# Rebuilding the second attention stage of a hybrid encoder layer: no PE transposes of the values, normalisation and gating moved out of the loop, values one step later

## Time and profile before

| | |
|---|---|
| median of 3 runs | 2778.05 us |
| profiled execution | 2780.88 us, span 2779.1 us |
| PE busy | 2647.0 us (95% of the span) |
| DVE / ACT / POOL busy | 1269.1 / 1065.1 / 373.8 us |
| DMA queue of SP | 362.03 MB, 48.8% of 16 engines |
| mean granted TensorE clock | 0.964 |

### The profile page before, as it was taken

The page is one execution under the profiler, slowest core; times in us unless marked ns, Lnnn a source line. Parts: engine busy times, 40 slices in busy tenths (PEclk is TensorE's granted clock), DMA queues, the critical chain, the costliest instruction groups (busy, mean ns, idle before and its releaser), DMA issues.

```text
span 2779.1 us, 39778 instructions
## 1 busy us (share of the span) xinstructions
PE 2647.0 (95%) x14546; PEld 2320.9 (84%) x14546; DVE 1269.1 (46%) x2638; ACT 1065.1 (38%) x2225; POOL 373.8 (13%) x257
## 2 busy tenths in 40 slices
PE   7999999999999999989999998884999999999997
PEld 5888888998888889989999988884788888888886
DVE  5211146141111363278877876786333433343333
ACT  4111122131111221278888877775222222222222
POOL 2000000000000000000000002333233233323331
PEclk9999999999999999999999987786999999999998
DMA  6431246363222363698876668766433333343330
GB/s 201 147 122 64 79 107 145 131 227 129 108 85 73 90 127 131 167 213 198 194 183 160 161 162 187 184 171 157 137 95 92 101 107 93 88 106 105 95 87 38
DMA packets 331191, 364.49 MB, mean 131 GB/s; under 512 B 83496, under 2 KB 253752, under 8 KB 326840
## 3 DMA queue, kind: packets, MB, share of 16 engines
q1 hardware_dynamic: 330168, 362.03, 48.8%
q0 software_dynamic: 896, 0.80, 0.1%
HBM read 227.88 MB, written 135.93 MB: 131 GB/s over the span
## 4 chain that ended last, share of the span: by engine, by line
PE 72%; issue 9%; DVE 9%; DMA 5%; SPq 2%; ACT 2%; POOL 1%; DVEq 0%; POOLq 0%; ACTq 0%
PE psum L1333 71%; DVE pt_lo L1143 5%; DMA g_b<-g_d 2%; DMA av<-v_d 1%; PE psum L1550 1%; POOL y_b L693 1%; DMA yb_d<-y_b 1%; DVE prob L1127 1%; DVE small L1127 1%; SPq L310 1%; SPq L438 0%; ACT prob_b L874 0%; PE psum L1496 0%; SPq L603 0%; DVE y_b L1208 0%
## 5 line engine op out<-in xcount | busy, mean ns | idle before, releaser
L1333 PE MATMUL psum<-x_hi,w_hi 128*128 128x512 f32 x1408 | 549.5, 390 | 18.4 <-DVE x_lo L1029 17.8
L1333 PE MATMUL psum<-x_lo,w_hi 128*128 128x512 f32 x1408 | 549.1, 390 | 0.0
L1333 PE MATMUL psum<-x_hi,w_lo 128*128 128x512 f32 x1408 | 549.0, 390 | 0.0
L693 POOL TENSOR_TENSOR y_b<-y_b,g_b 64x512 f32<-64x512 f32 x64 | 89.6, 1401 | 1776.2 <-DVE y_b L1208 1637.5
L1333 PEld LDWEIGHTS psum<-x_hi,w_hi 128*128 128x128 f32 x1408 | 265.1, 188 | 73.7 <-issue 17.8
L1333 PEld LDWEIGHTS psum<-x_lo,w_hi 128*128 128x128 f32 x1408 | 265.1, 188 | 55.2
L1333 PEld LDWEIGHTS psum<-x_hi,w_lo 128*128 128x128 f32 x1408 | 265.0, 188 | 54.9
L1127 DVE CUSTOM_DVE_ANT_0 prob<-psum,bias 128x640 f32<-128x640 f32 (+4 forms) x256 | 199.1, 778 | 86.2 <-issue 85.9
L1333 PE MATMUL psum<-wo_hi,y_hi 128*128 128x512 f32 x512 | 204.1, 399 | 31.9 <-DVE y_lo L1238 27.0
L839 ACT ACTIVATE prob<-prob,small 128x640 f32<-128x640 f32 (+4 forms) x256 | 204.0, 797 | 66.0 <-DVE small L1127 66.0
L1143 DVE TENSOR_TENSOR pt_lo<-psum,pt_hi 128x640 fp32r<-128x640 f32 (+4 forms) x256 | 199.2, 778 | 8.6 <-ACT pt_hi L848 8.6
(11 more groups left out here) (163 smaller groups left out, 5140.8 us busy)
## 6 DMA issues: line engine op xcount, KB each, us to landing
qk_d<-stage_out SPq DMA_DIRECT2D x80, 512.0 KB, 2.8
w_raw<-in_w_in SPq DMA_DIRECT2D x24, 1024.0 KB, 5.7
x_raw<-in_xT SPq DMA_DIRECT2D x32, 512.0 KB, 4.7
g_d<-stage_out SPq DMA_DIRECT2D x64, 256.0 KB, 2.0
bq_d<-stage_out SPq DMA_DIRECT2D x64, 256.0 KB, 4.0
v_d<-stage_out SPq DMA_DIRECT2D x32, 512.0 KB, 3.1
ya_d<-y_a SPq DMA_DIRECT2D x128, 128.0 KB, 3.6
bq<-bq_d SPq DMA_DIRECT2D x64, 256.0 KB, 4.3
```

The lines of the kernel that those rows point to most:

```text
L693: pool.tensor_tensor(yb, yb, g_b[:, s, :, :].rearrange("p h t -> p (h t)"), ALU.mult).then_inc(by_gated, 1)
L1333: return pe.matmul(dst, lhs, rhs, start=start, stop=stop)
```

## The change

Stage B is rebuilt, and what it took over from or leaves to its neighbours changes with it:

- Projection: the 8 A value heads and 2 B value heads are one block of 640 columns, two panels of 320, all token by feature into `v_d`. The B value units (4 per half, 512 wide) go; each of the 32 token-major products per half is 320 wide instead of 256.
- B loads its values straight from `v_d`, tokens on partitions, into a resident `v_b` (one 2 MB DMA per group instead of two of 0.5 MB); `b_v` and L889 go.
- Probabilities are no longer normalised. Row sums and shifts are kept for all units (`b_sum`, `b_shift`); after steps 50 and 66 the sink's exponential, sum and reciprocal are made for half of the sequence at once, transposed by PE and stored to `r_d`. Transposes wait for the exponentials alone.
- Values are made for two units at once (`b_values(d, part)`): per chunk three matmuls with 64 stationary and 256 moving columns, two chunks per step, at lags 7 and 8 from the first unit's scores (6 before). DVE copies a pair's output every second step (64x1024), SP stores it; POOL has nothing to do in B.
- C: gate and reciprocal are applied to all 8 column blocks in `y_tile`: two of POOL's three operations go from 512 to 1024 columns, `g_c` and `r_c` are twice as large. `mix(1)` moves ahead of PE's wait for all weight strips.
- Hand-over: tile 0 is loaded at step 57, tile 1 at step 61, eight strips before step 55; ACT and DVE split tile 0 at step 64 and one strip in each of steps 64 to 71.

```diff
-COL_QK, COL_G, COL_BQ, COL_BK, COL_BV, COL_AV = 0, 1024, 2048, 2560, 2688, 2816
+COL_QK, COL_G, COL_BQ, COL_BK, COL_V = 0, 1024, 2048, 2560, 2688
+V_HEADS = A_HEADS + B_KV
+VP = V_HEADS // 2
+VW = VP * HEAD
...
@@ SP
             def load_bv(kv, s):
-                for c in range(2):
-                    cols, src = kv_rows(ROW_BV, kv, s, c)
-                    sp.dma_start(bvt[c * HEAD:c * HEAD + HEAD, s, cols], src).then_inc(bv_loaded[s], 16)
...
+                sp.dma_start(v_b[:, s, n0:B_HALF // CHUNK, :].bitcast(f32),
+                             bass.AP(tensor=v_d.tensor, offset=first,
+                                     ap=[[row, P], [CHUNK * row, B_HALF // CHUNK - n0], [1, P]])
+                             ).then_inc(bv_loaded[s], 16)
...
+            def store_yb(d):
+                pair, s, i = b_unit(2 * d)
+                t0 = s * B_HALF + 4 * i * CHUNK
+                sp.wait_ge(by_copied, d + 1)
+                sp.dma_start(yb_d[pair * P:pair * P + 4 * HEAD, t0:t0 + 4 * CHUNK].rearrange("(h d) t -> d h t", d=HEAD),
+                             y_b[:, d % 2, :, :]).then_inc(by_stored[d % 2], 16)
...
+                if step == 3 * GROUP + 9:
+                    for stored in by_stored:
+                        sp.wait_ge(stored, 16 * (3 * B_UNITS // 2 + 1))
+                    sp.wait_ge(brecip_stored, 16 * 4)
                     load_tile(0, 0)
+                    load_x(0, 0)
+                if step == 3 * GROUP + 13:
+                    load_tile(1, 1)
+                if B_ALL + 4 <= step < B_ALL + 7:
+                    n = step - B_ALL + 4
+                    sp.wait_ge(cw_split, n - 4)
+                    load_strip(n)
...
+                if step >= 10 and step % 2 == 0 and step // 2 - 5 < B_DOUBLES:
+                    store_yb(step // 2 - 5)
+
+            sp.wait_ge(bvalues_done, B_DOUBLES)
+            for n in range(KT + 3, KT + 7):
+                load_strip(n)
+            for stored in by_stored:
+                sp.wait_ge(stored, 16 * (B_DOUBLES // 2 + 1))
+            load_strip(KT + 7)
...
@@ POOL
-                pool.tensor_tensor(y_raw[:, s, 0:KT // 2, :], y_raw[:, s, 0:KT // 2, :], g_c[:, s, :, :], ALU.mult
+                pool.wait_ge(y_loaded[s], 8 * (t - s) + 16)
+                pool.tensor_tensor(y_raw[:, s, :, :], y_raw[:, s, :, :], g_c[:, s, :, :], ALU.mult
                                    ).then_inc(y_ready, 1)
@@ ACT
-                    act.activation(small[:, 48 + 4 * q:52 + 4 * q], small[:, 16 + 4 * q:20 + 4 * q], ACT.Exp,
-                                   bias=sink_sb[:, 0, pair:pair + 1], scale=1.0).then_inc(bexp_done, 1)
...
-                    act.activation(v_b[:, u // 2 % 4, :, :].rearrange("p c d -> p (c d)"), psum[:, 7, :],
-                                   ACT.Copy).then_inc(bv_ready, 1)
...
-                    act.activation(yb_low[:, u % 2, :], psum[HEAD:P, 4 + u % 3, :], ACT.Copy).then_inc(by_low_ready, 1)
...
             for step in range(B_ALL + B_DRAIN):
                 b_step(step)
-                if B_ALL <= step < B_ALL + DRAIN_STRIPS:
+                if step == B_ALL:
+                    y_tile_hi(0, 0, True)
+                if B_ALL <= step < B_ALL + KT:
                     strip_hi(step - B_ALL)
@@ DVE (in b_step; denominator, reciprocal and normalisation per unit are gone)
+                if step % 2 == 1 and 0 <= step - 9 and (step - 9) // 2 < B_DOUBLES:
+                    d = (step - 9) // 2
+                    dve.wait_ge(bvalues_done, d + 1)
+                    dve.wait_ge(by_stored[d % 2], 16 * (d // 2 + 1))
+                    dve.tensor_copy(y_b[:, d % 2, :, :].rearrange("p h (c q) -> p h c q", q=CHUNK),
+                                    psum[0:HEAD, 4 + 2 * (d % 2):6 + 2 * (d % 2), :]
+                                    .rearrange("p a (c h q) -> p h (a c) q", h=4, q=CHUNK)).then_inc(by_copied, 1)
@@ PE
             def b_transpose(u):
-                pe.wait_ge(bnormed, u + 1)
+                pe.wait_ge(bexp_done, u + 1)
...
+            def b_values(d, part):
+                pair, s, i = b_unit(2 * d)
+                if part == 0:
+                    pe.wait_ge(bprobsT_split, 2 * d + 2)
+                    if d >= 2:
+                        pe.wait_ge(by_copied, d - 1)
...
+                for c in range(2 * part, 2 * part + 2):
+                    dst = psum[0:HEAD, 4 + 2 * (d % 2) + part, c % 2 * 2 * P:(c % 2 + 1) * 2 * P]
+                    ph, pl = (t[:, d % 3, c, :, :].rearrange("p u q -> p (u q)") for t in (ptb_hi, ptb_lo))
+                    vh, vl = (v_b[:, s, 4 * i + c, x:x + HEAD] for x in (0, HEAD))
+                    mm(dst, vh, ph, True, False)
+                    mm(dst, vh, pl, False, False)
+                    last = mm(dst, vl, ph, False, True)
...
             for step in range(-1, B_ALL + B_DRAIN):
-                for fn, lag in ((b_values, 6), (b_transpose, 3), (b_v, 3), (b_scores, -1)):
-                    if 0 <= step - lag < B_ALL:
-                        fn(step - lag)
+                v = step - 7
+                if 0 <= v < B_ALL:
+                    b_values(v // 2, v % 2)
...
+                if 0 <= step - 3 < B_ALL:
...
+                    b_transpose(step - 3)
+                if step + 1 < B_ALL:
+                    b_scores(step + 1)
...
             mix(0, 0)
             transpose_h(0, 0)
+            mix(1)
             pe.wait_ge(cw_split, 2 * KT + 2)
```

More of the change, by code:

```diff
@@ L395, in _ @@
                     if j == 1:
[L396 to L400 removed]
+                        next_panel(12, COL_V + VW, VW)
                 for w in range(2):
[L402 to L405 removed]
@@ L581, in _ @@
                     load_bk(1, group - 1, (since - 1,))
-                if group in (1, 2) and since == 5:
-                    sp.wait_ge(bv_done, B_UNITS * group)
+                if group in (1, 2) and since == 8:
+                    sp.wait_ge(bvalues_done, B_UNITS * group)
                     load_bv(1, group - 1)
@@ L773, in panel @@
                                 split_w(pbase + w + 1, i, 1 - slot, next_width)
-                        if last and half == 0:
-                            for c in x_after(r):
+                        if last and half == 0 and r % 2 == 1:
+                            for c in x_after(r // 2):
                                 split_x(1, c)
@@ L861, in _, with y_tile_hi, b_sinks, b_recip_copy @@
                            ).then_inc(recipT_copied, 1)
+            def y_tile_hi(t, s, first=False):
+                act.wait_ge(y_ready, t + 1)
+                if not first:
+                    act.wait_ge(mix_done, t)
+                act.activation(y_hi[:, :, :], y_raw[:, s, :, :], ACT.Copy).then_inc(y_hi_done, 1)
+            def b_sinks(s):
+                act.wait_ge(bexp_done, (3 + s) * 2 * B_UNITS)
+                for pair in range(B_HEADS // 2):
+                    cols = slice(s * P + pair * 32, s * P + pair * 32 + 32)
+                    last = act.activation(b_shift[:, cols], b_shift[:, cols], ACT.Exp, bias=sink_sb[:, 0, pair:pair + 1],
+                                          scale=1.0)
+                last.then_inc(bsink_done, 1)
+            def b_recip_copy(s):
+                act.wait_ge(brecipT_done, s + 1)
+                act.activation(recipb_t[:, s, :], psum[:, 3, 0:P], ACT.Copy).then_inc(brecipT_copied, 1)
             def b_step(step):
+                if step in (B_RECIP0, B_RECIP1):
+                    b_recip_copy(step == B_RECIP1)
                 u = step - 1
@@ L1239, in y_tile_lo @@
                                   ).then_inc(y_split, 1)
+            for step in range(B_ALL + B_DRAIN):
+                b_step(step)
+                if step == B_ALL:
+                    y_tile_lo(0, 0)
+                if B_ALL <= step < B_ALL + KT:
+                    strip_lo(step - B_ALL)
+            LN0 = CHAINED + 6
+            LN_STEPS = 8
             def p_tile_lo(t, s):
```

457 lines of the change are left out of this document (198 added, 259 removed).

## The result

The changed kernel takes 2739.83 us (median of 4 runs, 2737.41 to 2742.88); the kernel before, on the same chip, 2779.91 (2776.28 to 2782.74). The ratio is 0.9857, 95% interval 0.984 to 0.9874: 1.4% faster. The forecast was 2700 us, 2.8% faster, with a range of 2655 to 2745. The sign and the range held; the gain came out at half its size. The profiled execution took 2737.41 us, its span 2735.6.

A forecast was written before the change was run, and what follows sets the result against it. The prediction saw a chain of stalls in stage B and its hand-over, not one bound. Terms -2.5 - 48 - 29 + 1 = -78.5 took 2780.9 to 2702.4, less 2.8 for the median: 2700 us, range 2655 to 2745.

The forecast's parts named there:

- B's units, -48: Stage B's 64 units: 193 us in place of 241, from 155 for the first 48 and 38 for the last 16.
- The bound from compute: Stage B's loop over engines: 2.33 us per unit at full clock, 116 us for the first 48 units.
- DMA bound of 143: Stage B's first 48 units: moving 33.7 MB, values at 266 GB/s and the rest at 231, takes 143 us.
- the last 16: Stage B's last units: no keys or queries to wait for, 38 us with reciprocal block and tile loads.
- The bursts still stall it: Rival, chance 0.20: in stage B bulk loads ahead of stores keep DMA at 188 GB/s, 180 us; total 2725.
- The lag: Stage B: the values' added step of lag is hidden by their own slack and costs one step of drain.
- Drain, -29: From B's last exponentials to the start of mix(0, 0): 15 us in place of 44.
- Start of C, +1: From mix(0, 0) to the residual the second transposes need: +1 us, between -6 and +8.
- Stage C, 0: Stage C's loop: POOL's wider operations add 2.2 us a tile, within 3.1 of cover; 0.9 remain, 0 us.
- Stage C slips: Rival, chance 0.05: POOL slower by a factor of 2.2, each tile 6.4 us late, 192 us; total 2892.
- Stage A, "otherwise untouched": Stage A: only moved by a half of the projection moved into it, otherwise untouched; 0 us.
- Projection, -2.5: Projection on PE: B value units removed, 768 matmuls widened from 256 to 320 columns; -2.5 us for both halves.

The follow-up runs named there:

- e5: Changed kernel with stage B's later key and value loads spread over more steps in smaller DMAs, same bytes; 2730.23 us, ratio 0.9822.
- e10: Changed kernel plus DVE's residual first, ACT's waits swapped, one lag step less, B's loads spread, tile 2's loads earlier, PE's stage A loop written out; 2690.44 us.
- e6: Changed kernel without stage B's query, key and value loads after the first group (only its time counts); 2712.45 us, ratio 0.9750.
- e12: e10 with the loads of tiles 0 and 1 split over nine steps, r_c first, a store between them; 2686.58 us, ratio 0.9660.
- e11: e6 with the added step of lag in stage B undone as in e4 (only its time counts); 2703.28 us, ratio 0.9698.
- e4: Changed kernel with only the added step of lag in stage B undone; 2728.08 us, ratio 0.9812.
- e9: Changed kernel with tile 2's loads right behind the last strips and POOL's wait for constants moved to its first scaling; 2731.53 us, ratio 0.9808.
- e1: Changed kernel with ACT's y_hi waiting first for the mix, then for POOL's y; 2731.05 us, ratio 0.9814.
- e3: Changed kernel with 64 semaphore increments at the start of PE's program, moving stage A's loop down the code; 2734.11 us, ratio 0.9826.
- e8: Changed kernel plus DVE's residual first, ACT's waits swapped, one lag step less, tile 2's loads before the last two strips, PE's A loop written out; 2701.78 us.

## Why the prediction was right in stage B and wrong outside it

**B's units, -48: measured -46.3, by two errors that cancel, which is luck.** The bound from compute was sound: 2.35 us per unit without the loads against 2.33, and 113.7 us for the 48 units against 116. For the first 48 units 155 us were taken between a DMA bound of 143 and a ceiling; they took 140.9. That this is near 143 is luck too. The bound was priced at 231 GB/s, and it is none: spread, the same bytes moved at 247 GB/s and the 48 units took 129.4 us (e5) and 127.3 (e10), so the changed kernel loses 12 us there to its bursts. For the last 16, which "have no keys or queries to wait for", 38 us were taken, and they took 51. The forecast had tile 0's loads there only as something that might be late, not as something that holds up the output stores queued behind them. e6 and e12 show that stall. The rival *The bursts still stall it* had the right mechanism, but at 180 us for the 48 units a price far too high.

**The lag.** "The added step of lag for the values is hidden by their own slack": true of the steady loop (e11), but it counted the step at one step of drain, and it cost 4 us there and another 3 to 5 in the last units (e4, e11).

**Drain, -29: measured -25.1.** PE waited 5.0 us for a low part that stood behind tile 0's split and one weight strip, and DVE's work was not all as counted. Four strips were priced at 1.2 us each; the one here took 3.37 and the next 1.65, beside two operations of POOL on tile 1 that took 3.40 and 3.17 us in place of 2.34 (POOL, DVE, DVE, PE):

```profile
1858.81 3.40 POOL L727 TENSOR_TENSOR g_c<-g_c,r_c 128x1024 f32<-128x1024 f32 x1 [7.33 <-DMA r_c<-r_d]
...
1859.92 3.37 DVE L1240 TENSOR_TENSOR wo_lo<-strip_a,wo_hi 128x1024 fp32r<-128x1024 f32 x1
1863.22 0.68 DVE L1199 TENSOR_TENSOR ptb_lo<-psum,ptb_hi 128x512 fp32r<-128x512 f32 x1
...
1864.04 1.09 PE L1491 MATMUL psum<-ident,prob_b 128*128 128x128 f32 x4 [5.01 <-DVE ptb_lo L1199]
```

The prediction looked for DVE and POOL in each other's way in stage C, where POOL's operations keep their 2.39 to 2.40 us, and not in the drain, where the long operations stand side by side. In e9, where that strip takes 1.22 us and a later one 2.78, PE's longest wait is 4.0 us and the drain 18.6 in place of 19.2, so this explains a part of the 4 us; no run was made to take the two apart.

**Start of C, +1: measured +8.1.** The strips were all split 24.5 us after the start of `mix(0, 0)`, as predicted. But the prediction sets these 24.5 against 20.9 before and says that the rest follows as now, which makes +3.6; no working stands behind its +1. What also failed is "tile 2 and its three POOL operations follow as now": from there to tile 1's residual it took 26.6 us, not 21.1. POOL's two wider operations are 2.1 of that and the table load 1.3; the rest is put down to the loads, with twice as much for `g_c` and `r_c`, which is argued and not shown. That the second mix ahead wins nothing was right: tile 2's y stands in front of tile 1's residual on DVE.

**Stage C, 0: measured +9.8. This is the step that failed outright.** The cover of 3.1 us, the 2.2 us that POOL takes of it and the 0.9 that remain were read from an even tile. In an odd one the removed wait for `y_loaded` on ACT had changed which wait the table load stands behind, and 1.28 is more than 0.9 (e1: with the load back under the wait, 710.7 us). The rival *Stage C slips* looked at the right loop, but for a slower POOL; POOL's wide operations are 2.39 to 2.40 us in the rows above, as priced.

**Stage A, "otherwise untouched": measured +7.7.** Untouched source isn't untouched code: with 388 fewer PE instructions ahead of the loop, each jump back stalls PE twice in place of once (e3, e8).

**Projection, -2.5: measured +3.1.** The step of 320 columns was right: 0.147 us between two such matmuls. What was not counted: PE waits 4.8 us, 3 times, for `w_lo` (0.6 us before), and for 3.4 us its clock is low. The changed kernel and the twelve variants, all with this projection, end it between 1170.7 and 1175.3, so the size of this term is uncertain by 2 us; no run tested its cause.

Together: stage C and its start, taken at 0 and +1, are 17 of the 35 us that were missed, A 8, the projection 6, the drain 4. Two readings in the sum are slightly off and change nothing: the high copy on ACT is 0.60 us in the earlier trace rows, taken as 0.63, and the maxima take 0.71 from start to start in the earlier trace rows, taken as 0.60.

## What to carry to other kernels

When an engine gets a longer operation inside a loop, read every variant of the loop's turn (here odd and even tiles), and what the next engine does between the signal and its work: see in the trace which wait a table load stands behind, and where it stands behind the late signal, change the order of the waits (e1). When a change frees time in a stage, look at the queue that this stage shares with the next one's loads: here a small store behind large loads was the next stall (e5, e12). And compare the unchanged stages too: here a jump back cost PE 3 us or 6, by where the code stood.

## What the hardware showed beside this

- PE's weight loads stood 3.1 to 3.5 us after each of the two jumps back in a loop of some 1,980 instructions (the kernel before, e3); in the changed kernel its matmuls stood 6.0 and 5.6. There is no such stall where the three turns stand one behind the other (e8, e10, e12), and none where the loop is left: that branch takes 0.08 us in the changed kernel.
- An ACT table load of 1.28 us ran ahead of one of the waits written before its instruction, and behind the others. With two waits it was the last written (the changed kernel, e1). In the kernel before, with three (`y_loaded`, `y_ready`, `mix_done`), it was the middle one: its `y_hi` above waits for POOL behind the load. So the order in the source alone doesn't tell.
- A subtraction of DVE with both inputs in SBUF, 128x1024, took 3.37 us beside POOL's 128x1024 operation with two inputs, 1.2 alone; POOL's took 3.40 and 3.17, 2.34 alone. e4 (2.80 beside 3.37) and e9 (2.78 beside 3.68) show it too. Not every overlap lengthens DVE's part: in e9 another subtraction lies wholly beside the 3.68 us and takes 1.21.
- The copy above stood 8.84 us, from 1839.1 to 1847.9, for a store of 256 KB. From 1836 to 1841 the DMA engines had a share of 0.42 and moved 58 GB/s, so at first the bandwidth was not used up; from 1841 to 1848, with tile 1's first loads under way, it was 0.83 and 257 GB/s. Why this store took 12.6 us to land and the next 9.7, behind `r_c`'s broadcast loads of 512-byte rows (8.5 and 13.4 us), is not settled.
- Stage B's transfers moved 247 GB/s at a share of 0.99 when the loads were spread (e5).
